# Encoder memory turned by 32x32 transposes on VectorE instead of 128x128 turns on TensorE

## The reference

```
h = rms_norm(x, norm_mix_g)
x = x + (g_conv * conformer_conv(h) + g_mla * mla(h)) @ w_out
mem_n = rms_norm(mem, mem_norm_g)        # mem * rsqrt(mean(mem^2) + eps) * gain
q  = rms_norm(x, norm_mem_g) @ w_xq
kv = mem_n @ w_xkv                       # 2048 -> 4 heads of 128, keys and values
x = x + softmax(q k^T / sqrt(128)) v @ w_xo
x = x + relu(rms_norm(x, norm_ffn_g) @ w_ff1)^2 @ w_ff2
```

## Time and profile before

| | |
|---|---|
| median of three runs | 1644.53 us |
| profiled execution, span from first to last instruction | 1641.9 us |
| TensorE busy | 1625.8 us, 99% |
| VectorE busy | 1088.7 us, 66% |
| ScalarE busy | 810.6 us, 49% |
| granted TensorE clock, mean | 0.999 |

### The profile page before, as it was taken

The page is one execution under the profiler, slowest core; times in us unless marked ns, Lnnn a source line. Parts: engine busy times, 40 slices in busy tenths (PEclk is TensorE's granted clock), DMA queues, the critical chain, the costliest instruction groups (busy, mean ns, idle before and its releaser), DMA issues.

```text
span 1641.9 us, 22070 instructions
## 1 busy us (share of the span) xinstructions
PE 1625.8 (99%) x7612; PEld 1360.0 (83%) x7612; DVE 1088.7 (66%) x1480; ACT 810.6 (49%) x1061; POOL 97.9 (6%) x187
## 2 busy tenths in 40 slices
PE   9999999999999999999999999999999999999998
PEld 7888888888888888888888888888888888888886
DVE  5688988888888898665555655555555555545554
ACT  6444456555555556744445644434443444334443
POOL 6500011211111000000000000000000000000000
PEclk9999999999999999999999999999999999999999
DMA  7666655655555665557564566566656665566654
GB/s 250 204 187 187 191 158 159 176 168 180 170 160 172 219 198 186 187 184 262 176 199 135 153 182 191 190 193 191 185 187 193 192 184 185 193 192 186 191 186 141
DMA packets 160992, 304.78 MB, mean 186 GB/s; under 512 B 11657, under 2 KB 19969, under 8 KB 160513
## 3 DMA queue, kind: packets, MB, share of 16 engines
q1 hardware_dynamic: 159552, 299.41, 59.2%
q0 software_dynamic: 1056, 3.46, 0.6%
q10 hardware_dynamic: 320, 1.06, 0.2%
HBM read 301.78 MB, written 2.10 MB: 185 GB/s over the span
## 4 chain that ended last, share of the span: by engine, by line
PE 96%; ACT 2%; DVE 1%; issue 0%; DMA 0%; SPq 0%; ACTq 0%
PE ps L1328 29%; PE ps L1330 29%; PE ps L1329 29%; PE ps L1341 2%; PE ps L1512 1%; PE ps L1511 1%; ACT hconv L759 0%; DVE wlo L893 0%; ACT whi L544 0%; PE ps L1528 0%; PE ps L1601 0%; PE ps L1600 0%; PE ps L1599 0%; PE ps L1522 0%; DMA x_in<-in_x_dram 0%
## 5 line engine op out<-in xcount | busy, mean ns | idle before, releaser
L893 DVE TENSOR_TENSOR wlo<-raw,whi 128x1024 fp32r<-128x1024 f32 x560 | 686.1, 1228 | 413.9 <-ACT whi L544 408.9
L544 ACT ACTIVATE whi<-raw 128x1024 fp32r<-128x1024 f32 x560 | 591.7, 1060 | 566.2 <-PE ps L1330 555.7
L1328 PE MATMUL ps<-whi,a_hi 128*128 128x512 f32 x1212 | 477.9, 394 | 0.0
L1330 PE MATMUL ps<-whi,a_lo 128*128 128x512 f32 x1212 | 472.3, 390 | 0.0
L1329 PE MATMUL ps<-wlo,a_hi 128*128 128x512 f32 x1212 | 471.9, 389 | 0.0
L1328 PE MATMUL ps<-whi,c_hi 128*128 128x512 f32 x752 | 293.8, 391 | 0.0
L1330 PE MATMUL ps<-whi,c_lo 128*128 128x512 f32 x752 | 292.7, 389 | 0.0
L1329 PE MATMUL ps<-wlo,c_hi 128*128 128x512 f32 x752 | 292.6, 389 | 0.0
L1330 PEld LDWEIGHTS ps<-whi,a_lo 128*128 128x128 f32 x1212 | 227.5, 188 | 47.8
L1328 PEld LDWEIGHTS ps<-whi,a_hi 128*128 128x128 f32 x1212 | 227.7, 188 | 45.7 <-DVE wlo L893 0.2
L1329 PEld LDWEIGHTS ps<-wlo,a_hi 128*128 128x128 f32 x1212 | 227.8, 188 | 45.5
(11 more groups left out here) (254 smaller groups left out, 1169.4 us busy)
## 6 DMA issues: line engine op xcount, KB each, us to landing
raw<-in_w_ff_dram SPq DMA_DIRECT2D x256, 512.0 KB, 3.9
raw<-in_w_in_dram SPq DMA_DIRECT2D x144, 512.0 KB, 3.8
raw<-in_w_mla_out_dram SPq DMA_DIRECT2D x32, 512.0 KB, 4.5
raw<-in_w_conv_out_dram SPq DMA_DIRECT2D x32, 512.0 KB, 4.4
raw<-in_w_out_dram SPq DMA_DIRECT2D x32, 512.0 KB, 4.5
raw<-in_w_ukv_dram SPq DMA_DIRECT2D x16, 512.0 KB, 3.7
raw<-in_w_xkv_dram SPq DMA_DIRECT2D x16, 512.0 KB, 4.3
raw<-in_w_uq_dram SPq DMA_DIRECT2D x16, 384.0 KB, 3.8
```

The source lines that it names most:

```text
L544: act.activation(whi[:, s, :], raw[:, s, :], ACT.Copy).then_inc(hi_ready, 1)
L893: dve.tensor_tensor(wlo[:, s, :], raw[:, s, :], whi[:, s, :].bitcast(F32), ALU.subtract).then_inc(lo_ready, 1)
L1328: pe.matmul(sum_, x_hi[:, k0 + k, tok], w_hi, start=(first and k == 0), stop=False)
L1330: mm = pe.matmul(sum_, x_lo[:, k0 + k, tok], w_hi, start=False, stop=(last and k == kts - 1))
```

## The change

`mem` no longer goes through `rows` and TensorE. It is loaded in four blocks of 64 tokens (two times 32). A block's buffer `mem_blk` holds, on partitions 32j to 32j+31, 32 tokens of the columns 512j to 512j+511, for j = 0 to 3. One VectorE instruction transposes all of its 32x32 blocks into `m_turn`, reading every 16th value of a row, so that partition p holds the columns 16p to 16p+15. The rows of `w_xkv` and the gain are put in the same order by how they are loaded. `m_hi` and `m_lo` are made from `m_turn` (in SBUF) in chunk 2, two tiles in each k, `m_lo` over `m_turn` itself. For the sums of squares, the whole `mem` is loaded a second time into `mem_row`, and ScalarE squares it in two instructions in chunk 3.

```diff
+MEM_AT = ((0, 2), (0, 6), (1, 2), (1, 6))
+    w_xkv = w_xkv.rearrange("o (p k) n -> p (o k) n", p=P)
+    mem_blocks = mem.rearrange("o (q i r) (j n) -> q j r (o i) n", q=4, i=2, j=4)
-        sq_mem = at(o + KS + KS // 2, "sq_mem", [P, TT, NC])
+        mem_row = at(o, "mem_row", [P, TT, D])              # over a_hi
+        m_turn = at(o + KS, "m_turn", [P, KT, SEQ])         # over m_lo
+        mem_blk = at(o, "mem_blk", [P, 2, 2, NC])           # over rows
@@ gpsimd, start
+            pool.dma_start(mem_g[:], mem_norm_g.rearrange("o (p k) -> p (o k)", p=P)).then_inc(mem_g_landed, 16)
-            for n, v in enumerate((conv_ln_g, conv_ln_b, norm_mem_g, mem_norm_g, norm_ffn_g)):
+            for n, v in enumerate((conv_ln_g, conv_ln_b, norm_mem_g, norm_ffn_g)):
@@ gpsimd, memory
                 if c >= 2:
-                    pool.wait_ge(turned, 2 * (T_MEM + c - 1))
-                    pool.wait_ge(ss_ready, SS_KV + TT * (c - 1))
-                pool.dma_start(rows[:, c % 2, :, :], mem_v[:, :, NC * c:NC * (c + 1)]).then_inc(mem_landed[c % 2], 16)
+                    pool.wait_ge(mem_turned, c - 1)
+                for j in range(4):
+                    pool.dma_start(mem_blk[32 * j:32 * (j + 1), c % 2, :, :], mem_blocks[c, j]).then_inc(mem_landed[c % 2], 16)
+                if c == 1:
+                    pool.dma_start(mem_row[:], mem_v).then_inc(mem_row_landed, 16)
@@ scalar
-                    if k == 2:
-                        act.wait_ge(mem_landed[c % 2], 16 * (c // 2 + 1))
-                        chunk_squares(sq_mem, rows[:, c % 2, :, :], c, SS_KV + TT * c)
-                        turn_out(T_MEM + c, m_hi, 4 * c, V_MEMN)
+                    if c == 2:
+                        if k == 0:
+                            act.wait_ge(mem_turned, 4)
+                            act.wait_ge(mem_g_landed, 16)
+                        for n in (2 * k, 2 * k + 1):
+                            last = act.activation(m_hi[:, n, :], m_turn[:, n, :], ACT.Copy, scale=mem_g[:, n:n + 1])
+                        last.then_inc(m_high, 1)
+                    if c == CH - 1 and k < TT:
+                        if k == 0:
+                            act.wait_ge(mem_row_landed, 16)
+                        act.activation(mem_row[:, k, :], mem_row[:, k, :], ACT.Square, accum_out=ss_sum[:, k:k + 1]).then_inc(ss_ready, 1)
-            act.wait_ge(sum_ready, 1)
+            act.wait_ge(ss_ready, SS_MEM)
@@ vector
-                    if k == 2:
-                        turn_low(T_MEM + c, m_lo, m_hi, 4 * c, V_MEMN)
+                    if (c, k) in MEM_AT:
+                        q = MEM_AT.index((c, k))
+                        dve.wait_ge(mem_landed[q % 2], 64 * (q // 2 + 1))
+                        dve.transpose(m_turn[:, :, 64 * q:64 * (q + 1)].rearrange("p k (i r) -> p k i r", i=2),
+                                      mem_blk[:, q % 2, :, :].rearrange("p i (c k) -> p k i c", k=KT)).then_inc(mem_turned, 1)
+                    if c == 2:
+                        dve.wait_ge(m_high, k + 1)
+                        for n in (2 * k, 2 * k + 1):
+                            last = dve.scalar_tensor_tensor(out=m_lo[:, n, :], in0=m_turn[:, n, :], scalar=mem_g[:, n:n + 1],
+                                                            in1=m_hi[:, n, :].bitcast(F32), op0=ALU.mult, op1=ALU.subtract)
+                        last.then_inc(m_low, 1)
-                    elif k == 4:
-                        add_parts(SS_MEM, 1)
-                    else:
+                    elif k > 4:
                         centre(k - 5)
@@ tensor
-            pe.wait_ge(vec_landed, 16 * 7)
+            pe.wait_ge(vec_landed, 16 * 6)
-                    if k == 2:
-                        pe.wait_ge(mem_landed[c % 2], 16 * (c // 2 + 1))
-                        turn(T_MEM + c, rows[:, c % 2, :, :], 0, split_out(T_MEM + c - 1) if c else None)
-                        pe.wait_ge(turn_lo, 2 * splits_before(T_MEM) + k + 1)
+                        pe.wait_ge(m_low, k + 1)
```

More of the change, by code:

```diff
@@ L74 @@
 T_CKV = T_CQ + 1
-T_MEM = T_CKV + 1
-T_XK = T_MEM + CH
+T_XK = T_CKV + 1
 T_MRG = T_XK + 1
@@ L108 @@
 SS_KV = SS_Q + TT
-SS_MEM = SS_KV + TT * CH
+SS_MEM = SS_KV + TT
 SS_1 = SS_MEM + TT * CH
@@ L126 @@
 XO_BANK = (4, 0, 2, 4)
+MEM_AT = ((0, 2), (0, 6), (1, 2), (1, 6))
 def pair_of(n):
     return (n + 1) % 2
-V_MIX, V_LG, V_LB, V_NMEM, V_MEMN, V_FFN = (KT * n for n in range(6))
-V_QG = 6 * KT
+V_MIX, V_LG, V_LB, V_NMEM, V_FFN = (KT * n for n in range(5))
+V_QG = 5 * KT
 V_KG = V_QG + LT
@@ L176, in build @@
     w_in, w_uq, w_ukv, w_mla_out, w_conv_out, w_out = (k_rows(w) for w in (w_in, w_uq, w_ukv, w_mla_out, w_conv_out, w_out))
-    w_xq, w_xkv, w_xo, w_ff1, w_ff2 = (k_rows(w) for w in (w_xq, w_xkv, w_xo, w_ff1, w_ff2))
+    w_xq, w_xo, w_ff1, w_ff2 = (k_rows(w) for w in (w_xq, w_xo, w_ff1, w_ff2))
+    w_xkv = w_xkv.rearrange("o (p k) n -> p (o k) n", p=P)
+    mem_blocks = mem.rearrange("o (q i r) (j n) -> q j r (o i) n", q=4, i=2, j=4)
     x_v, mem_v, out_v = (v.rearrange("o (t p) n -> p (o t) n", p=P) for v in (x, mem, out))
@@ L267, in build @@
         pos_i = take("pos_i", [P, TT], I32)
+        mem_g = take("mem_g", [P, KT])
         assert cursor[0] <= nc.sbuf_usable_end, (cursor[0], nc.sbuf_usable_end)
@@ L324, in build @@
         mem_landed = [sem("mem_landed0"), sem("mem_landed1")]
+        mem_row_landed, mem_g_landed, mem_turned, m_high, m_low = (sem(n) for n in ("mem_row_landed", "mem_g_landed", "mem_turned", "m_high", "m_low"))
         gated, res_landed = sem("gated"), sem("res_landed")
@@ L813, in _ @@
                 if k == 2:
-                    act.wait_ge(sum_ready, 2)
+                    act.wait_ge(sum_ready, 1)
                     root(sd_n, ss_sum, D)
@@ L845, in ff_group @@
                         if first and c == 0 and k == 4:
-                            act.wait_ge(sum_ready, 3)
+                            act.wait_ge(sum_ready, 2)
                             root(sd_n, ss_sum, D)
```

## The result

The kernel after takes 1651.37 us (median of 4, 1649.64 to 1651.76); before 1644.44 us (median of 4). The ratio is 1.0039, interval 1.0027 to 1.0051: slower by more than the 0.2% that can be told from no change, and above my range of 1640.8 to 1648.0 us. The profiled run took 1651.13 us with a span of 1648.5; before's span was 1641.9. The difference of 6.6 us is taken apart here.

What follows compares the result with a forecast made beforehand. TensorE (99% busy) bounds the kernel, with VectorE's list deciding: 4.1 us gained less 1.9 us of waiting at the mean gives 2.3 us, so 1644.5 - 2.3 = 1642.2 us; range 1640.8 to 1648.0 us.

Steps and rivals of the forecast that it cites:

- TensorE's side: Up to the LayerNorm's mean, TensorE saves 3.8 us of turns and 0.3 us of waiting, 4.1 us if nothing else is late.
- VectorE's side: VectorE's instruction list in w_mla_out delays the mean to 622.5, 1.9 us of new waiting, leaving a gain of 2.3 us.
- The transpose: Four new 128x1024 transposes on VectorE, each taken at 1.13 us of pitch, bounded between 0.6 and 6.5 us.
- The rule that I weighed: Trainium skill's cacheline note: crossing into another 16-byte line is penalised, steps up to four fp32 are free; no figure given.
- rival 2: 15%: strided transposes are slow in chunks 0 and 1; 1646.7 us at twice the pitch, deciding from 1.7 us upward.
- The load step: First memory block, four 128 KB DMAs, lands at 551.0 to 552.5, taken as 551.5; its transpose ends at 552.6.
- 6.6 us fits with hardly a margin; I count nothing: Chunk 0 weight units landing in 6.6 us, due after about 7, cost nothing; 0 to 1.5 us kept for the range.
- rival 3: 13%: loads are late, 2.5 MB more on GpSimd's queue beside the weights; 2 to 4 us, giving 1644.2 to 1646.2.
- S: Time from the first matmul of w_mla_out to the LayerNorm's mean; 83.07 us before, 80.74 predicted.
- (1,6): Chunk 1, unit 6 of w_mla_out: VectorE is 0.2 us late here and never waits again from here on.
- Before the mean TensorE doesn't stop: In w_mla_out, TensorE gets every `lo` in time up to the LayerNorm's mean, so no waits there.
- the 0.7 us of slack that I found for (3,3): Chunk 3, unit 3: its `lo` ends at 614.5 and is wanted by TensorE at 615.2.

Runs made afterwards that it cites:

- e12: The kernel of e9 with the m_hi and m_lo pairs moved once more, all behind the additions of the mean; 1642.69 us, ratio 0.9993.
- e4: The kernel after, its four transposes reading with steps of 16, 8, 4 and 2 values and writing side by side; one run, 1650.75 us.
- e10: The kernel before, each chunk of mem loaded by four transfers of 32 partitions in place of one over 128; 1649.14 us, ratio 1.0029.
- e11: The kernel before plus the second 2 MB load of mem, with nothing computed on it; 1644.83 us, ratio 0.9999.
- e2: The kernel after, with the second load of mem and its squares covering only 64 of the 2048 columns; 1647.61 us, ratio 1.0022.
- e9: The kernel after, with transposes later, m_hi/m_lo pairs spread, the second load in four pieces behind all block loads, squares at (3,5) and (3,6); 1643.05 us, ratio 0.9992.
- e1: The kernel after, each transpose reading 32 values side by side instead of every 16th; 1650.08 us, ratio 1.0031.
- e6: The kernel after, with only the four transposes moved later, to (0,5), (1,1), (1,4) and (1,7); 1649.12 us, ratio 1.0032.
- e3: The kernel after, with all m_hi and m_lo made in the last four units of chunk 3, behind the mean; 1645.74 us, ratio 1.0004.
- e7: The kernel after, with the second 2 MB load split into four spaced pieces between the blocks, squared at (3,5) and (3,6); 1657.67 us, ratio 1.0078.
- e5: The kernel after, with transposes later, m_hi/m_lo pairs spread, two transfers per block, and row pieces between the blocks; 1648.86 us, ratio 1.0026.
- e8: The kernel after, each memory block loaded by two transfers over 128 partitions instead of four over 32; 1652.61 us, ratio 1.0049.

## Why the prediction was wrong

**TensorE's side held.** 4.1 us were to be had up to the mean; e12 shows 4.16. What failed is VectorE's side: three terms of its sum were too small, and together they turned a gain of 2.3 us into a loss.

**The transpose was mis-sized.** Four pitches of 1.89 in place of 1.13 make 3.0 us more on VectorE. I chose the nearest row by size and type, and no row had the step. The rule that I weighed had the right sign, and rival 2 its condition (1.7 us and over); by itself this term would have made 1645.2 us, within my range. The rule's threshold is off: "SBUF — State Buffer" in the Trainium skill gives four fp32 values of step for free, e4 shows two free and four at the full price. The same note's "≥2 hits per line" fits: with a step of 2 each 16-byte line serves two values, with 4 only one.

**The load step failed in its first half.** I had the block landing at 551.5 from four issues beside an unchanged landing time of 4 to 4.7 us. The issues were as assumed, 0.55 us each (eight in 4.37 us), so the fourth went out at about 547.4. But the block was there 6.3 us after that: the transpose began at 553.73, 1.9 us late when the later start of the stage is taken off. e10 shows the late landing on the kernel before, 7.2 us after the first issue in place of 4.7. Why transfers over 32 partitions land later wasn't found.

**The sentence "6.6 us fits with hardly a margin; I count nothing" failed by combination.** With blocks in quarters and 2 MB behind them ScalarE waited for weights and passed 2.0 us of it on to VectorE (0.95 + 1.01). Either one alone did less harm: e11 has 13.0 us landings, 4.3 us of ScalarE's waits and 3.8 of VectorE's for `whi`, but VectorE has the idle time for them there; e2, without the 2 MB, has no wait of VectorE for `whi`. The total of ScalarE's waits decides nothing: e9 still has 12.4 us and e12 20.5 us of them, and no stop inside the chunks. A smaller slip of rival 3: the software queue moved 5.55 MB in place of 3.46, so 2.1 MB more and not 2.5.

These terms, 3.0 + 1.9 + 2.0 = 6.9 us, are nearly the 7.2 us between predicted and measured S (80.74, 87.96). This sum is read from VectorE's list in one trace. As predicted, VectorE never rests after (1,6), in fact from 570.8 us on, and every microsecond of lateness reached the mean. Taken away singly the terms returned less than their size: by S, e1 gained 0.3 us for 3.0 removed, e2 1.55, e6 1.3 for 3.57; in e1 and e6 longer waits of VectorE for blocks and weights refilled the place. By the medians e1 and e6 are 5.7 and 4.5 us above before, against 6.9 after, so the sizes are rough. What undid them together was the room: with VectorE's work placed elsewhere (e3) S fell by 4.8 us, with block loads apart as well (e9, e12) by 6.7 and 9.05.

**"Before the mean TensorE doesn't stop" was wrong.** It waited for `wlo` inside the chunks, 1.49 us at 570.91, 0.44 at 574.36 and 1.30 at 622.05. With VectorE 7 us late, the 0.7 us of slack that I found for (3,3) was gone.

**Behind the mean nothing returns, but 1.4 us were added** by the clock near 890 us. It comes and goes with and without the change: on the kernel before, e10 and e11 have the fall (0.67 from 885 to 890 us in e11) and the profiled run of before doesn't; of the versions of the kernel after, e1, e3, e6, e7 and e12 don't have it, while after, e2, e4, e5, e8 and e9 do. The 0.3 us ahead of the stage are less than what its start differs by from run to run. So about 4.9 us of the span's 6.6 belong to the change. What decides whether the clock falls is open. In the medians (6.9 us) it is mixed in with both kernels.

Rivals 2 and 3 were each priced, and each at its mild end would have lain within my range. They came together. The upper end of the range, 1648.0, had 4.5 us for the transposes and so only 1.3 for the loads; the loads took 1.9 + 2.0. The miss of 9.2 us is 7.2 in S, 0.3 ahead of it, 1.4 by the clock and 0.3 between span and time. Two rows misled: 1.13 us of pitch and 4.7 us of landing were both "nearest rows", of operations that differ from the new ones in just the property that counted.

## What to carry to other kernels

- When work moves to an engine that is at 93% in a stage, price every new operation there by its access pattern too, and add the rivals' prices before setting the range: without idle time all of them reach the end together.
- Cutting a load into quarters has a price of its own: here 7.2 us until all of it was there, in place of 4.7, with the same bytes. What that costs depends on who waits: 4 us of S in e10, where TensorE did. Whole rows of 2 MB more cost nothing on the kernel before, where the engines had slack, but 1.55 us of S or more where VectorE was already late.
- The room in a list matters more than the prices. The same slow transposes, quarter loads and 2 MB made S 4.9 us longer than before's packed into chunks 0 to 2, and 1.9 (e9) and 4.2 us (e12) shorter with the work placed where VectorE had time.
- Work moved behind one meeting point is work ahead of the next: of e12's 4.16 us at the mean the span kept 2.1.

## What the runs showed of the hardware

- VectorE's 32x32 transpose of 128x1024 fp32 takes 1.24 us with source steps of 1 or 2 values, and 1.9 to 2.1 us with 4, 8 or 16 (e1, e4, after; one transpose each for 2, 4 and 8).
- On GpSimd's queue eight loads of 128 KB over 32 partitions need 4.4 us to issue; the first four, which make up a chunk, were complete 7.2 us after the first issue (e10), 8.0 in the kernel after; a single load of 512 KB over 128 partitions after 4.7 us. A load of 256 KB whose source has four entries in its slowest dimension took 11.1 us (e8).
- TensorE came back at the lower clock after stops of 1.8 us (e3, for 3 us), 2.5 us (e10, 3 us), 3.7 us (e5, 6 us) and 9.4 us (e7, 4 us), so that a stop cost up to twice its length. A stop doesn't always do this: after 3.46 us in e8 (at 561.03) and after the 2.2 us at the mean in after, e1, e2, e6, e8 and e9 the granted clock stayed at 2.4 GHz. After 2.4 us of idle at the softmax it came back at either level, in different runs.
